# The low parts of 71 weight units made by VectorE where GpSimd made them

## What is computed

```python
y_a = hgrn2_mixer(hq, hf, hi, hg, lower_bounds[l], hg_norm_g[l]) @ w_hg_o[l]
y_b = mla_mixer(cq, ckv, kpe, q_a_norm_g[l], w_q_b[l], kv_a_norm_g[l], w_kv_b[l], cos, sin) @ w_mla_o[l]
gate_a, gate_b = jnp.split(jax.nn.sigmoid(gates + b_gate[l]), 2, axis=-1)
mixed = (gate_a * y_a + gate_b * y_b) @ w_out[l]
h = h + rms_norm(mixed, mix_post_g[l])
...
gt, up = jnp.split(u @ w_ffn_in[l], 2, axis=-1)
h = h + rms_norm((jax.nn.silu(gt) * up) @ w_ffn_out[l], ffn_post_g[l])
```

```python
mix = jnp.concatenate([_merge(o_moba), _merge(o_nsa), _merge(o_diff), _merge(o_swa)], axis=-1)
x = x + _rms_norm(mix @ w_out[l], attn_post_norm[l])
h = _rms_norm(x, ffn_pre_norm[l])
a = lax.conv_general_dilated(h @ w_gate, ...) + conv_b
x = x + _rms_norm((jax.nn.gelu(a, approximate=True) * (h @ w_up)) @ w_down, ffn_post_norm[l])
```

## Time and profile before

| | |
|---|---|
| median of 3 runs | 920.56 us (920.22 to 921.38) |
| the profiled execution | 920.36 us, span 918.6 us |
| TensorE busy | 900.7 us, 98% of the span |
| VectorE busy | 670.3 us, 73%, 1279 instructions |
| ScalarE busy | 466.5 us, 51% |
| GpSimd busy | 208.5 us, 23%, 114 instructions |
| granted TensorE clock | 0.997 of 2.4 GHz |
| DMA | 153.67 MB, mean 167 GB/s |

### The profile page before, as it was taken

How to read it: one execution, slowest core, us unless ns; L and a number is a source line. 1 busy time by engine, 2 the same in 40 slices (tenths; PEclk the granted TensorE clock), 3 DMA queues, 4 the chain that set the end, 5 groups by cost and what they waited for, 6 DMA issues and landing times.

```text
span 918.6 us, 16815 instructions
## 1 busy us (share of the span) xinstructions
PE 900.7 (98%) x6767; PEld 799.8 (87%) x6767; DVE 670.3 (73%) x1279; ACT 466.5 (51%) x937; POOL 208.5 (23%) x114
## 2 busy tenths in 40 slices
PE   8999999999999999999999999999999999999997
PEld 8879999889999888888888799887988888888886
DVE  6625987657656888766676768867888888788885
ACT  7443336564443574434444647776744345543443
POOL 4123421541212210652314342221110210210110
PEclk9999999999999999999999999999999999999999
DMA  8535443334343655655545354324546445465441
GB/s 323 193 138 184 140 162 117 115 112 135 122 137 122 229 175 189 226 184 204 194 160 221 137 192 152 109 91 151 193 144 224 167 178 212 178 225 188 175 146 46
DMA packets 23181, 153.67 MB, mean 167 GB/s; under 512 B 2864, under 2 KB 3248, under 8 KB 5568
## 3 DMA queue, kind: packets, MB, share of 16 engines
q1 hardware_dynamic: 22384, 150.43, 46.1%
q0 software_dynamic: 576, 2.10, 0.6%
q10 hardware_dynamic: 144, 0.07, 0.0%
HBM read 151.28 MB, written 1.05 MB: 166 GB/s over the span
## 4 chain that ended last, share of the span: by engine, by line
PE 90%; ACT 5%; DVE 4%; issue 1%; DMA 0%; DVEq 0%; ACTq 0%
PE pb L507 88%; ACT FA L513 2%; PE pb L510 2%; DVE FA L516 1%; ACT wh L513 1%; ACT R L513 1%; DVE X L522 1%; DVE wl L516 1%; DVE R L522 1%; ACT L513 0%; DVE st L519 0%; DVE FA L525 0%; ACT st L513 0%; DMA FA<-in_meta 0%; DVE st L534 0%
## 5 line engine op out<-in xcount | busy, mean ns | idle before, releaser
L507 PE MATMUL pb<-R,wh 128*128 128x256 f32 (+2 forms) x2224 | 550.3, 326 | 4.6 <-ACT R L513 2.0
L507 PE MATMUL pb<-R,wl 128*128 128x256 f32 (+1 forms) x1512 | 422.6, 281 | 0.0
L507 PEld LDWEIGHTS pb<-R,wh 128*128 128x128 f32 x2224 | 372.3, 190 | 43.7 <-ACT R L513 3.5
L516 DVE TENSOR_TENSOR wl<-raw,wh 128x1024 fp32r<-128x1024 f32 (+1 forms) x204 | 269.2, 1342 | 85.0 <-ACT wh L513 83.3
L516 POOL TENSOR_TENSOR wl<-raw,wh 128x1024 fp32r<-128x1024 f32 (+1 forms) x74 | 180.0, 2437 | 623.6 <-ACT wh L513 500.8
L507 PEld LDWEIGHTS pb<-R,wl 128*128 128x128 f32 x1512 | 284.3, 188 | 2.2 <-issue 0.5
L513 ACT ACTIVATE wh<-raw 128x1024 fp32r<-128x1024 f32 (+1 forms) x220 | 223.8, 1044 | 52.7 <-PE pb L507 50.0
L507 PE MATMUL pb<-wh,R 128*128 128x512 f32 (+2 forms) x724 | 234.1, 388 | 1.3 <-ACT R L513 1.1
L507 PEld LDWEIGHTS pb<-wh,R 128*128 128x128 f32 (+1 forms) x724 | 134.4, 186 | 33.4 <-ACT R L513 1.5
L513 ACT ACTIVATE FA<-pb 128x256 f32<-128x256 f32 (+7 forms) x240 | 94.2, 415 | 123.2 <-PE pb L507 112.1
L507 PE MATMUL pb<-wl,R 128*128 128x512 f32 (+2 forms) x372 | 143.4, 385 | 0.0
(11 more groups left out here) (122 smaller groups left out, 458.6 us busy)
## 6 DMA issues: line engine op xcount, KB each, us to landing
raw<-in_w SPq DMA_DIRECT2D x137, 1024.0 KB, 4.8
X<-in_x SPq DMA_DIRECT2D x2, 512.0 KB, 4.1
raw<-in_w SPq DMA_DIRECT2D x2, 512.0 KB, 6.7
post<-in_ffn_post SPq DMA_DIRECT2D x2, 512.0 KB, 4.6
post<-in_w POOLq DMA_DIRECT2D x2, 512.0 KB, 5.0
FA<-in_w POOLq DMA_DIRECT2D x2, 512.0 KB, 7.6
out<-X SPq DMA_DIRECT2D x4, 256.0 KB, 2.0
cst<-in_cst SPq DMA_DIRECT2D x1, 821.5 KB, 12.5
```

What stands on the lines that cost most here:

```text
L507: return self.real.matmul(*a, **k) if self.real else self
L516: return self.real.tensor_tensor(*a, **k) if self.real else self
```

## The change

71 letters of `MADE` change: 55 times p becomes d and 16 times q becomes v. The high part stays in each case with the engine that made it (ScalarE for the 55, VectorE for the 16); the low part goes from GpSimd to VectorE. Nothing else changes: same units, same `ORDER`, same buffers. GpSimd keeps the halves of units 0 and 1 (which `FIRST` and `HALF` set) and its other work.

```diff
--- before.py
+++ after.py
@@ -410,9 +410,9 @@
-MADE = ("dpdpddddddddqdpdpdddpddpvpvdppqpdddppddddpddvqpqpqpdpdvddpdddpqddvdpddppddpddpddpddvvdddqvddddpd"
-        "ddvvvdvdppdpdppvvpdqpdpqvddpvpdvpdddvpdvpdvdddvqdddqqpddpdpvddvdddddddpvvvdppvpppdvvdddvpdqddddd"
-        "pvddvddddvdddvdpqpdddddddqddddddddddddddppddpddddddqddddvddvdvddddddpdvvdddvdvpddddd")
+MADE = ("dpdpddddddddvdddddddddddvdvdddvdddddddddddddvvdvdvddddvdddddddvddvdddddddddddddddddvvdddvvdddddd"
+        "ddvvvdvddddddddvvddvdddvvdddvddvddddvddvddvdddvvdddvvddddddvddvddddddddvvvdddvddddvvdddvddvddddd"
+        "dvddvddddvdddvddvddddddddvdddddddddddddddddddddddddvddddvddvdvddddddddvvdddvdvdddddd")
```

## The result

The changed kernel took 945.2 us (median of four executions, 943.76 to 949.31), the kernel before 920.39: a ratio of 1.0271, 95% interval 1.0259 to 1.0283. Forecast were 942.0 us and a range of 932 to 951. The profiled execution was the longest of the four, 949.31 us with a span of 947.5.

The account below looks back on a forecast made before the run. TensorE, busy 98% of the span, was taken to bound the kernel. Waits of 18.4 us and 3 us for the clock on 920.36 us gave 941.8, or 942.0 us on the median of 920.56; range 932 to 951 us.

Parts of the forecast that it names:

- The load: VectorE overall: 87 us of low parts added, 25 to 60 us back from stretched instructions, sum 697 to 732 us.
- Where the cover holds: Scan, both feed-forward stages, first block's head attention: extra 1.22 us hidden beside TensorE's work; some 50 units cost 0.6 us together.
- The eleven places: VectorE's queue at units 52, 88, 154, 166, 171, 172, 174, 175, 176, 184, 186: TensorE waits, 18.35 us including covered units.
- the last stretch: Units 184 and 186, ahead of op steps: low parts exceed VectorE's idle time, 1.2 and 0.65 us.
- Units 52, 154 and 172: Ahead of o_scale, an op step and scores of swa 1: TensorE waits 1.5, 2.0 and 2.9 us more.
- Units 174, 175 and 176: At the fourth transpose, value of swa 0 and second half of 24 matmuls: 2.8, 1.8 and 2.6 us.
- unit 166: Score steps held back by 4.2 us, mostly hidden by other waits of TensorE: 0.9 us.
- Unit 171: Score steps held back by 2.7 us, mostly hidden by other waits of TensorE: 0.75 us.
- The clock: TensorE behind five new idle times of 2.4 to 2.9 us: near two clock drops, 3 us, from 0 to 8.5.
- B: Rival: most is absorbed, later waits come free, half stays and the clock doesn't fall; 930 us, chance 0.11.
- C: Rival: faster, as VectorE's instructions stretched by GpSimd vanish, some 3 us in second block's attention; 917.5 us, chance 0.04.
- D: Rival: VectorE becomes the bound over whole stretches, about eight windows adding 1 to 3 us each; 955 us, chance 0.06.

Follow-up runs that it names:

- the kernel with the eleven left out: The changed kernel, but units 52, 88, 154, 166, 171, 172, 174, 175, 176, 184, 186 keep low parts on GpSimd: 921.43 us, ratio 1.0006.
- both parts on VectorE: The kernel before, with the high and the low part of unit 172 made by VectorE: 924.2 us, ratio 1.0032.
- the kernel with the eleven alone: The kernel before, only low parts of units 52, 88, 154, 166, 171, 172, 174, 175, 176, 184, 186 moved to VectorE: 949.21 us, ratio 1.0309.
- the second four: The changed kernel itself, measured once more with no edit and with its own profile: 949.87 us, ratio 1.0318.

## Why the prediction was right, step by step

- **The load.** Forecast 697 to 732 us for VectorE, near 710; it is 692.2. Added were 71 x 1.223 = 86.8 us, so 670.3 + 86.8 - 692.2 = 65 us came back from stretched instructions (62 us if the durations are added up, since busy time counts an overlap once), more than my upper bound of 60. No low part took over 1.3 us; 18 had taken over 1.5. The term was mis-sized and had no effect on the sum: the time given back lay in VectorE's waits.
- **Where the cover holds.** Right: no change in the feed-forward stages; the 60 moves outside the eleven places cost 0.06% with an interval that holds zero. One small cost showed, 0.36 us at units 80 to 83, in both profiles of the changed kernel; it is missing in the kernel with the eleven left out, which moves unit 80 as well, so that move alone doesn't make it.
- **The eleven places.** The sum was right, covered ones included: 18.35 us forecast, 18.2 measured in the first profile and 17.5 in the second (or in the first without the trade in the last stretch). Units 52, 154 and 172 were right within 0.05 us. Units 174, 175 and 176 were 0.25 to 0.45 us too high. The one large miss is unit 166: 0.9 forecast, 1.7 measured. I had seen that the two score steps come 4.2 us later and took it that other waits hide most of that; there were none, TensorE had no idle time in the whole stretch before. Unit 171 was 0.25 too high. The last stretch grew by 1.74 us for 1.85 forecast. That the sum is nearer than its terms is luck in part: 0.8 us too low at one place, some 1.6 us too high at the others together.
- **What the wait is.** Half right. The times of the high parts' ends were read rightly, but the text made it a wait for ScalarE. With both parts on VectorE 2.26 of the 2.89 us remained: the way round starts at TensorE's own last use of the place.
- **The clock.** This is the step that failed. Forecast 3 us, bound 8.5; measured 10.4 in the first profile and 11.2 in the second. The price of a fall was right (up to 1.7 forecast, 1.2 to 1.8 measured, but for unit 166 with 1.9 to 3.4), though the fall it was read from cost nothing itself. Their number was wrong: near two forecast, six stretches with slower work in the first profile, in the second and in the kernel with the eleven alone. My reason for two, that other waits cover part of the slower work, holds in the last stretch and at none of the six. I had counted five idle times of 2.4 to 2.9 us, which doesn't fit my own terms either: unit 175 stood there with 1.8 us (measured 1.74), and unit 154 adds its 2.5 to the 0.80 already there (measured 3.24). And 2.16 us at unit 52 (the old 0.71 and the new 1.45) and 1.7 us at unit 166 brought falls too, and the earlier trace rows had shown one behind 1.45 us. The first four executions show the spread: 943.76 and 944.06 us at a clock of 0.991, 946.35 at 0.986, 949.31 at 0.985.
- **The range.** The median of the first four executions is 24.8 us above the kernel before, that of the second four 29.2 us. With 17.5 us of idle time, as in the profiles, that leaves an estimated 7 and 12 us for the clock. The second is over its bound of 8.5, and the time stayed under 951 us only because the idle times stayed 4 us under theirs. That is luck; one of those four executions, 951.53 us, didn't stay under it.
- **The rule on the clock.** By the rule of the Trainium skill ("TensorE: Matmul & The Clock Gate", section "What's actually happening") the clock is a matter of how busy the array has lately been. The traces agree in the direction: every stretch with slower work lies behind an idle time. The 26.9 us that I put beside that rule (28.95 measured in the profiled execution) is no statement of the section. It is my 18.4 us of waits and five times the price from the earlier trace rows; that each of the five would bring a fall was my guess.
- **The rivals.** B is out: nothing was absorbed but the 0.44 us behind unit 154 that the sum had counted. C is out by its own mechanism, at the one place where it was tried alone, unit 171 (the stretched instruction went and TensorE gained 0.0 us), and over the 60 moves outside the eleven places. D is out: 60 of the 71 moves cost nothing. The rule of the Trainium skill named with C ("SBUF — State Buffer", section "Who interferes with whom") holds in these traces, 2.34 us for an instruction of 0.17 that ends with GpSimd's; but it brought no gain where it was lifted, and a loss of 1.66 us where a shift led into it.

## What to carry to other kernels

Before moving work onto an in-order engine, ask for each piece what it waits for, what stands right behind it, and whether the engine that bounds the kernel needs that next: eleven of 71 moves made the whole loss, and where they stood decided it, not how much work they were. Trace the wait to its root; if the operand's buffer is given back by the very engine that will stand, the whole chain from there on is exposed. Price an idle time of TensorE with the fall of its clock behind it, unless another wait stands behind to take the slower work up, and after any shift look again for collisions with the engine that shares a resource.

## What was not expected of the hardware

- A 128 x 2 instruction on VectorE took 2.34 us in place of 0.17 when it began 0.03 us after a GpSimd tensor_tensor, and ended with it. It lost 2.17 us; the most that a low part of 1.22 us lost in the kernel before is 2.2 us (it took 3.42).
- Some 65 us of such stretching in the kernel before were worth nothing in time that could be measured.
- A fall of TensorE's clock cost 1.2 to 1.9 us at most of the eleven places, 0.6 to 0.8 us at 328 us, and nothing at one, where TensorE would have waited 1.53 us for ScalarE without it.
- The same program, with the same idle times of TensorE within 0.1 us, had its clock fall behind units 52 and not 176 in one execution, and behind 176 and not 52 in another; the difference between sets of four executions (945.2 and 949.87 us) is larger than that between most of the kernels above. Whether both sets ran on the same chip is not on record.
